# Last output tile in parts of 384 and 128 tokens, last token tile sent in two halves of columns

## What is computed

```python
def swiglu(h, w_in, w_out):
    gate, up = jnp.split(h @ w_in, 2, axis=-1)
    return (jax.nn.silu(gate) * up) @ w_out
...
        x = x + 0.5 * gate[:, 2, None, :] * swiglu(h, ffn2_w_in[l], ffn2_w_out[l])
    return rms_norm(x, final_g)      # x * rsqrt(mean(x*x, -1) + eps) * final_g
```

## Time and profile before

| | us |
|---|---|
| median of 3 runs | 1849.14 (1848.89 to 1849.58) |
| the profiled execution | 1850.24 |
| its span | 1848.4 |
| PE busy in the span | 1828.7 (99%) |
| DVE busy | 1045.4 (57%) |
| ACT busy | 732.7 (40%) |
| granted TensorE clock, mean | 0.999 |

### The profile page before, as it was taken

The page is one execution under the profiler, slowest core; times in us unless marked ns, Lnnn a source line. Parts: engine busy times, 40 slices in busy tenths (PEclk is TensorE's granted clock), DMA queues, the critical chain, the costliest instruction groups (busy, mean ns, idle before and its releaser), DMA issues.

```text
span 1848.4 us, 25278 instructions
## 1 busy us (share of the span) xinstructions
PE 1828.7 (99%) x9424; PEld 1513.1 (82%) x9424; DVE 1045.4 (57%) x1512; ACT 732.7 (40%) x1273; POOL 219.4 (12%) x278
## 2 busy tenths in 40 slices
PE   8999999999999999999999999999999999999998
PEld 6888778777888888888888888888888888888887
DVE  6896857665577843333346797556334763333332
ACT  5345434565333432233224763335232443222332
POOL 1110041000010400000011255053000100000010
PEclk9999999999999999999999999999999999999999
DMA  8965833211476333333333433313334333333331
GB/s 314 303 192 157 248 105 91 69 47 41 137 247 203 91 95 98 102 91 89 108 90 115 137 103 88 88 29 87 102 96 153 91 91 102 95 98 88 110 93 52
DMA packets 350216, 218.89 MB, mean 118 GB/s; under 512 B 39965, under 2 KB 334186, under 8 KB 349486
## 3 DMA queue, kind: packets, MB, share of 16 engines
q1 hardware_dynamic: 338006, 173.22, 32.9%
q0 software_dynamic: 11504, 40.79, 6.5%
q10 hardware_dynamic: 616, 3.67, 0.5%
HBM read 208.83 MB, written 9.99 MB: 118 GB/s over the span
## 4 chain that ended last, share of the span: by engine, by line
PE 93%; DVE 4%; ACT 2%; issue 1%; DMA 0%; DVEq 0%; SPq 0%; ACTq 0%
PE psum L446 27%; PE psum L448 27%; PE psum L447 26%; PE psum L1713 2%; PE psum L1511 1%; PE psum L1541 1%; PE psum L1418 1%; PE psum L1402 1%; PE psum L1522 1%; PE psum L1606 0%; DVE delta_qkv_T L2551 0%; DVE act_lo L2551 0%; DVE ada_sum L2551 0%; PE psum L974 0%; PE psum L1223 0%
## 5 line engine op out<-in xcount | busy, mean ns | idle before, releaser
L446 PE MATMUL psum<-act_hi,w_hi 128*128 128x512 f32 (+1 forms) x1624 | 647.2, 399 | 2.6 <-DVE act_lo L2551 1.4
L448 PE MATMUL psum<-act_hi,w_lo 128*128 128x512 f32 (+1 forms) x1624 | 630.0, 388 | 0.0
L447 PE MATMUL psum<-act_lo,w_hi 128*128 128x512 f32 (+1 forms) x1624 | 629.5, 388 | 0.0
L411 DVE TENSOR_TENSOR w_lo<-w_raw,w_hi 128x1024 fp32r<-128x1024 f32 x304 | 379.9, 1253 | 281.4 <-ACT w_hi L403 259.4
L403 ACT ACTIVATE w_hi<-w_raw 128x1024 fp32r<-128x1024 f32 x304 | 317.5, 1052 | 186.3 <-PE psum L448 166.7
L446 PEld LDWEIGHTS psum<-act_hi,w_hi 128*128 128x128 f32 x1624 | 305.2, 188 | 68.3 <-issue 6.2
L448 PEld LDWEIGHTS psum<-act_hi,w_lo 128*128 128x128 f32 x1624 | 305.0, 188 | 63.6
L447 PEld LDWEIGHTS psum<-act_lo,w_hi 128*128 128x128 f32 x1624 | 305.5, 188 | 59.7 <-issue 1.4
L446 PE MATMUL psum<-ffn_hi,w_hi 128*128 128x512 f32 (+1 forms) x396 | 145.8, 368 | 0.0
L448 PE MATMUL psum<-ffn_hi,w_lo 128*128 128x512 f32 (+1 forms) x396 | 144.8, 366 | 0.0
L447 PE MATMUL psum<-ffn_lo,w_hi 128*128 128x512 f32 (+1 forms) x396 | 144.8, 366 | 0.0
(11 more groups left out here) (419 smaller groups left out, 2268.8 us busy)
## 6 DMA issues: line engine op xcount, KB each, us to landing
w_raw<-in_ffn_w_in SPq DMA_DIRECT2D x88, 512.0 KB, 3.7
w_raw<-in_w_in SPq DMA_DIRECT2D x68, 512.0 KB, 3.8
w_raw<-in_mix_w_in SPq DMA_DIRECT2D x52, 512.0 KB, 3.8
ada_w<-in_ada_w POOLq DMA_DIRECT2D x48, 512.0 KB, 5.2
w_raw<-in_ffn_w_out SPq DMA_DIRECT2D x32, 512.0 KB, 3.8
late_ada_w<-in_ada_w POOLq DMA_DIRECT2D x24, 512.0 KB, 4.8
w_raw<-in_ffn_w_out SPq DMA_DIRECT2D x16, 384.0 KB, 3.4
w_raw<-in_w_branch_a SPq DMA_DIRECT2D x8, 512.0 KB, 4.7
```

The source lines that it names most:

```text
L411: dve.tensor_tensor(WLO[:, n % 4, :], RAW[:, n % 4, :], WHI[:, n % 4, :].bitcast(F32), ALU.subtract).then_inc(w_lo, 1)
L446: pe.matmul(out, whi, hhi, start=start, stop=False)
L447: pe.matmul(out, whi, hlo, start=False, stop=False)
L448: return pe.matmul(out, wlo, hhi, start=False, stop=stop)
```

## The change

A table `LAST_PARTS = ((0, 3), (3, 4))` gives the token tiles of each part of the last output tile: part 0 has 384 tokens (token tiles 0 to 2), part 1 has 128 (tile 3). Matmuls, sums, transposes, residual sum, squares, means and roots follow it. Token tile 2's 896 columns are scaled by ScalarE right after part 0's root, and SP sends the whole tile as its third transfer. Of token tile 3, ScalarE scales columns 0 to 511 and sends them (ACT's queue); VectorE scales columns 512 to 895 and the last 128 from PSUM, waits for its own work, and signals; SP sends columns 512 to 1023.

```diff
--- before.py
+++ after.py
@@ -564,6 +564,7 @@
 
         FIRST_T = 5
         X_TURN_AT = (2, 4, 5, 6)
+        LAST_PARTS = ((0, 3), (3, 4))
         RELAID = 16 + 16 * (P // SUB) * NT
         INVERSE_LOADS = (7, 14, 21, 28)
         BPH = T // SUB
@@ -790,10 +791,10 @@
             for n in (0, 1):
                 sp.wait_ge(sem("out_T_taken"), KD + n)
                 sp.dma_start(ov[:, n, :], YTOK2[:, n, :]).then_inc(stored, 16)
+            sp.wait_ge(sem("final_x"), KD + 1)
+            sp.dma_start(ov[:, 2, :], YTOK2[:, 2, :]).then_inc(stored, 16)
             sp.wait_ge(sem("out_T_taken"), KD + 2)
-            sp.dma_start(ov[:, 2, 0:D - P], YTOK2[:, 2, 0:D - P]).then_inc(stored, 16)
-            sp.wait_ge(sem("out_T_taken"), KD + 3)
-            sp.dma_start(ov[:, 2:4, D - P:D], YTOK2[:, 2:4, D - P:D]).then_inc(stored, 16)
+            sp.dma_start(ov[:, 3, D // 2:D], YTOK2[:, 3, D // 2:D]).then_inc(stored, 16)
             sp.wait_ge(stored, 16 + 16 * 5)
 
 
@@ -1270,24 +1271,25 @@
                 else:
                     pe.wait_ge(sem("squares_ready"), NT + 8 * 4 + half)
                 slot = square_slot(4, KD - 1) if part else 0
-                for n in (0, 1):
-                    tok = slice((2 * half + n) * P, (2 * half + n) * P + P)
-                    mm = pe.matmul(PS[:, 4, 2 * half + n:2 * half + n + 1], SQ[:, slot, tok], ONES[:, 0:1],
-                                   start=(part == 0 and n == 0), stop=(part == 1 and n == 1))
+                n0, n1 = LAST_PARTS[half]
+                for n in range(n0, n1):
+                    tok = slice(n * P, n * P + P)
+                    mm = pe.matmul(PS[:, 4, n:n + 1], SQ[:, slot, tok], ONES[:, 0:1],
+                                   start=(part == 0 and n == n0), stop=(part == 1 and n == n1 - 1))
                 if part == 0:
                     return
                 mm.then_inc(sem("square_sum"), 1)
-                pe.wait_ge(sem("final_x"), KD + half)
+                pe.wait_ge(sem("final_x"), KD + 2 * half)
                 pe.wait_ge(sem("out_T_taken"), KD - 3 + half)
-                for n in range(2):
-                    tok = slice((2 * half + n) * P, (2 * half + n) * P + P)
-                    mm = pe.transpose(PS[:, 6 + half, n * P:n * P + P], XT[:, KD - 1, tok], ID)
+                for n in range(n0, n1):
+                    tok = slice(n * P, n * P + P)
+                    mm = pe.transpose(PS[:, 6 + half, (n - n0) * P:(n - n0) * P + P], XT[:, KD - 1, tok], ID)
                 mm.then_inc(sem("out_T"), 1)
 
             def last_tile(pl):
 
                 for half in range(2):
-                    tok = slice(256 * half, 256 * half + 256)
+                    tok = slice(P * LAST_PARTS[half][0], P * LAST_PARTS[half][1])
                     bank = pe_open(pe, pl, 7 + half)[:, tok]
                     for c, (k0, kn) in enumerate(((0, 8), (8, 8), (16, 6))):
                         n = pl.chunk + 21 + c
@@ -1936,7 +1938,8 @@
             def last_taken(pl):
 
                 for half in range(2):
-                    tok = slice(256 * half, 256 * half + 256)
+                    n0, n1 = LAST_PARTS[half]
+                    tok = slice(P * n0, P * n1)
                     act.wait_ge(x_ready, NORM_X[4] + half)
                     act.wait_ge(sem("squares_added"), 6 * 3 + KD - 1 - 3)
                     act.activation(SQ[:, square_slot(4, KD - 1), tok], XT[:, KD - 1, tok], ACT.Square)\
@@ -1946,11 +1949,13 @@
                     if half == 0:
                         out_taken(KD - 2)
                     act.wait_ge(sem("mean_recip"), NT + 4 + half)
-                    act.activation(col(RCOL + 2 * half, 2), col(RCOL + 2 * half, 2), ACT.Sqrt).then_inc(sem("rms_ready"), 1)
-                act.wait_ge(sem("rms_ready"), NT + 5)
-                copy(YTOK2[:, 3, 0:D - P], YTOK2[:, 3, 0:D - P], scale=col(RCOL + 3)).then_inc(sem("final_x"), 1)
-                act.wait_ge(sem("final_x"), KD + 2)
-                act.dma_start(out[0, 3 * P:4 * P, 0:D - P], YTOK2[:, 3, 0:D - P]).then_inc(stored, 16)
+                    act.activation(col(RCOL + n0, n1 - n0), col(RCOL + n0, n1 - n0), ACT.Sqrt).then_inc(sem("rms_ready"), 1)
+                    act.wait_ge(sem("rms_ready"), NT + 4 + half)
+                    act.wait_ge(sem("out_T_taken"), KD - 1)
+                    scaled = YTOK2[:, n1 - 1, 0:D // 2 if half else D - P]
+                    copy(scaled, scaled, scale=col(RCOL + n1 - 1)).then_inc(sem("final_x"), 1)
+                act.wait_ge(sem("final_x"), KD + 3)
+                act.dma_start(out[0, 3 * P:4 * P, 0:D // 2], YTOK2[:, 3, 0:D // 2]).then_inc(stored, 16)
 
             def out_stage(name, r, per_tile, after=None):
 
@@ -3484,25 +3489,27 @@
             residual("ffn2_out", 3, MOD + 48 + 16)
             pl, f = Place("ffn2_out", 0), KD - 1
             for half in range(2):
-                tok, mine = slice(256 * half, 256 * half + 256), slice(2 * half, 2 * half + 2)
+                n0, n1 = LAST_PARTS[half]
+                tok, mine = slice(P * n0, P * n1), slice(n0, n1)
                 dve.wait_ge(chunk_done, pl.chunk + 22 + half)
                 chained(stt(XT[:, f, tok], PS[:, pl.bank(f + half), tok], col(MOD + 48 + 16 + f), XT[:, f, tok], ALU.mult, ALU.add))
                 dve.sem_inc(x_ready, 1)
-                rcol = col(RCOL + 2 * half, 2)
+                rcol = col(RCOL + n0, n1 - n0)
                 dve.wait_ge(sem("square_sum"), 2 * 3 + 1 + half)
                 chained(ts(rcol, PS[:, 4, mine], 1.0 / D, EPS, ALU.mult, ALU.add))
                 dve.reciprocal(rcol, rcol).then_inc(sem("mean_recip"), 1)
                 dve.wait_ge(sem("rms_ready"), NT + 4 + half)
                 dve.wait_ge(sem("out_T_taken"), KD - 1)
                 if half:
-                    ts(YTOK2[:, 2, 0:D - P], YTOK2[:, 2, 0:D - P], col(RCOL + 2), None, ALU.mult).then_inc(sem("out_T_taken"), 1)
+                    mine_of = YTOK2[:, 3, D // 2:D - P]
+                    cnt.mark(ts(mine_of, mine_of, col(RCOL + 3), None, ALU.mult))
                 dve.wait_ge(sem("out_T"), KD + half)
-                last = tt(YTOK2[:, mine, D - P:D], PS[:, 6 + half, 0:256].rearrange("p (n d) -> p n d", d=P), b3(rcol, P), ALU.mult)
+                cnt.mark(tt(YTOK2[:, mine, D - P:D], PS[:, 6 + half, 0:P * (n1 - n0)].rearrange("p (n d) -> p n d", d=P),
+                            b3(rcol, P), ALU.mult))
+                cnt.wait()
                 if half:
-                    last.then_inc(sem("out_T_taken"), 1)
+                    dve.sem_inc(sem("out_T_taken"), 1)
                 else:
-                    cnt.mark(last)
-                    cnt.wait()
                     for n in (0, 1):
                         ts(YTOK2[:, n, 0:D - P], YTOK2[:, n, 0:D - P], col(RCOL + n), None, ALU.mult).then_inc(sem("out_T_taken"), 1)
```

## The result

The changed kernel takes 1855.46 us (median of 8 runs, 1854.93 to 1857.08); the kernel before, beside it, 1849.49 (8 runs). The ratio is 1.0032, with a 95% interval of 1.0023 to 1.0041: slower by 6.0 us, clear of noise. The forecast was 1.2 us more, too little to be told from no change. The medians are those of all runs; the ratios follow the means.

The account below looks back on a forecast made before the run. The prediction took matmul issue time on TensorE (93% of the chain) as the bound. It summed +3.1 for TensorE's end, -0.5 to the scaling, -0.3 for it and -1.1 for transfers to +1.2 us: median 1850.3, range 1847.3 to 1852.5.

Parts of the forecast that it names:

- TensorE's end: End of TensorE's work on the last output tile: 3.5 - 0.7 + 0.5 - 0.2 = +3.1 us.
- Part 0, +3.5: Last tile's part 0, 384 wide in place of 256: 66 matmuls at 0.173 us, not 0.120, +3.5 us.
- Part 1, 0.109 a step, -0.7: Last tile's part 1, 128 wide: weight loading sets 0.109 us for each of 66 matmuls, -0.7 us (bounds -1.5 and 0).
- The small matmuls, +0.5: Part 0's sums and transposes amid part 1: twelve passes and three transposes, not eight and two, +0.5 us at 0.098 each.
- The opening sums of part 1, -0.2: Part 1's opening sums on TensorE: four passes become two, -0.2 us.
- What lies beside it, 0: VectorE's and ScalarE's added work on part 0 falls before part 1 ends, over 2 us staying free: cost nothing.
- The tail, -0.5 and -0.3: After TensorE's end, one token tile left: -0.5 us up to the scaling, -0.3 us for the scaling itself.
- The transfers, -1.1: Final transfers: only 0.52 MB left in two issues, landing 2.5 us after the last issue, -1.1 us.
- number 2: Part 1's narrow matmuls fall back to two passes, 0.236 us each: +7.7 in place of -0.7, 1858.7 us; 15%.
- Rivals 1: Part 1's loading hides, columns alone count: 0.067 us a matmul, 1847.5 us, 5%; at 81 ns 1848.4 us, 7%.
- 3: Early transfers run into the last ones: last half tile waits up to 0.9 us on one engine, 1851.2 us; 7%.
- 4: Tail does not shorten as the diff says: VectorE's chain sets the last issue, landing is fixed; +1.1, 1851.4 us; 2%.

Follow-up runs that it names:

- stream_192: The changed kernel with part 1's matmuls streaming 192 tokens, 64 of them read by nobody: 1851.66 us against 1849.79 for the kernel before, ratio 1.0009.
- wide_stream: The changed kernel with part 1's matmuls streaming 256 tokens, token tile 2 computed once more and unread: 1852.28 us against 1849.92 for the kernel before, ratio 1.0013.
- early_sums: The changed kernel with part 0's opening sums moved into part 0, amid matmuls of 384 tokens: 1851.60 us against 1850.16 for the kernel before, ratio 1.0008.
- after_short_sums: The changed kernel without part 0's opening sums, 6 passes in place of 12: 1850.65 us against 1849.79 for the kernel before, ratio 1.0006.
- after_again: The changed kernel itself, measured on another occasion: 1855.82 us against 1849.79 for the kernel before, ratio 1.0028.
- wide_then_narrow: The changed kernel with part 1's first 24 matmuls streaming 256 tokens, the other 42 streaming 128: 1852.88 us against 1849.92 for the kernel before, ratio 1.0014.
- narrow_then_wide: The changed kernel with part 1 streaming 256 tokens for 3 matmuls, 128 for 21, 256 for 42: 1852.35 us against 1849.92 for the kernel before, ratio 1.0012.
- narrow_long_sums: The kernel before, part 1 streaming 128 tokens (token tile 2's products omitted), sums lengthened to 12 passes, 3 transposes: 1854.04 us against 1849.79, ratio 1.0016.

## Why the prediction was wrong

**The step that failed** is the term of TensorE's end, +3.1 us, and in it the pace of 0.109 us for all 66 narrow matmuls and of 0.098 for the sums between them. Each pace was read from rows at full clock, and the prediction never asks whether the clock stays up in the stretch that it makes; no term and no rival allows for a fall. The runs showed in its place a granted clock of 0.50 from about 1838.4 us on, 42 narrow matmuls at 0.213 us, and a TensorE's end of +8.45 us (1841.02 to 1849.47).

Point by point:

- *Part 0, +3.5*: measured +3.6. The pace of 384 lies halfway between those of 256 and 512: 0.173.
- *Part 1, 0.109 a step, -0.7*: at full clock right (0.110 for 24, 0.112 in `stream_192`'s steps with half as many columns more), as the load of the weights would have it. The other 42 ran at 0.213, which alone is 42 x (0.213 - 0.109) = +4.4. The rule in "TensorE: Matmul & The Clock Gate" of the Trainium skill that prices such a pair at about 81 ns ("Back-to-back issue gap") is not borne out here; the one in "LDWEIGHTS (loading the stationary operand)", columns / 1.2, is: 107 ns against 110 to 112.
- *The small matmuls, +0.5*: right at full clock (in `wide_stream` the block runs from 1837.53 to 1839.07 us, 1.54 against 0.98 + 0.5), +1.3 where the clock fell in their midst. The opening sums of part 1, -0.2: measured 0.0 at half clock.
- *What lies beside it, 0*: right. VectorE was idle for 7.30 us before the last residual sum, and the transfers of tiles 0 to 2 were over by 1848 us, 4 us before the last issue.
- *The tail, -0.5 and -0.3*: in `wide_stream` -0.46 to the scaling and -0.3 for it, as forecast; in the change -0.6 in all, since its two closing passes ran at half clock (0.59 us against 0.38 in `wide_stream`).
- *The transfers, -1.1*: right (-1.1), 2.1 and 2.6 us from issue to landing.
- *The sum*: with the clock held, +1.2 was forecast; `early_sums` measured +1.4, `wide_stream` +2.4 where 1.9 was expected of it, each to within some 1.8 us. The difference to the change, 6.0 less 1.4, gives an estimate of 4.6 us for the clock.

Of the rivals, number 2 named a time on the right side for the wrong reason. Its 0.236 us a step is near the 0.213 measured, and a reader who looks at the slow steps alone would take it for confirmed. Three things speak against it: the first 24 narrow steps take 0.110, each matmul has one record, and the clock column says 0.50. Rivals 1, 3 and 4 found nothing: no pace under 0.110, and no transfer in the way.

How the loss arises is shown as far as this. That the clock was halved is seen in the profile. That narrow matmuls and the long row of passes must come together is seen on one chip: with either one changed alone, `stream_192` or `after_short_sums`, no run in ten fell, against nine in ten of the change. In both profiled falls of the change (1838.4 us, and 1837.9 in `after_again`) the clock fell within the passes, so the transposes and the narrow matmuls behind them cannot have brought it about there; the one profiled fall of `wide_then_narrow` came behind the sums, at 1840.1 us. That in the same kernel some runs fall and others don't (6 of 10) is not explained by any run here, nor why `narrow_then_wide` never fell; nor is it shown how much of either is needed, beyond the kernels in the table.

In these three falls TensorE had work in each instant before. The Trainium skill ("TensorE: Matmul & The Clock Gate", Part 1, "What's actually happening") says that the default is the throttled clock and activity releases it. The two levels seen here agree; the default no row here shows, since the profile lists 1.00 from its start (0 to 8 us, where TensorE has no work yet). That a TensorE which is never idle but moves few columns can lose the clock is what these runs add.

## What to carry to other kernels

Narrowing a matmul that has weights of its own to load can save little time (0.120 to 0.110 us for half the columns here), and it can cost the clock: before narrowing a stretch, look for other thin work inside it (here sums with one moving column), since both together halved the clock and cost more than the shorter tail gained. Small matmuls whose inputs are ready early are better placed amid wide ones: moved there, the same instructions ran 4 to 5 us faster. And in any forecast for TensorE, write down the granted clock that each pace was read at, as a term that can change.

## What the runs showed of the hardware

- Moving columns and pace of a matmul with its own 128 x 128 weights of type fp32r, full clock: 512: 0.226 us, 384: 0.173, 256: 0.120, 192: 0.112, 128: 0.110. At a granted clock of 0.50, 128: 0.213.
- TensorE's granted clock went from 1.00 to 0.50 with TensorE busy all the time (at about 1838.4 us, amid the passes), and did not come back in the 9.6 us of narrow matmuls that followed (1839.8 to 1849.4).
- The same program on the same chip fell in some runs and not in others: 6 of 10 for `narrow_long_sums`, 9 of 10 for `after_again`. A single profile would have told the wrong story of two kernels here: `wide_then_narrow` (it fell in the profile and in no other run) and `narrow_long_sums` (the reverse of most).
- Two transfers of 256 KB issued together landed 2.1 and 2.6 us after issue, where 448, 448 and 128 KB, issued within 0.4 us, took 2.5, 3.4 and 3.6.
